# The masks of a blockwise triangular inverse: applied by VectorE as each level's product leaves PSUM, in place of GpSimd's masked copies ahead of it

## The reference

```python
def wkv_step(S, inp):
    r_t, w_t, k_t, v_t, a_t, b_t = inp
    sa = jnp.einsum('bhij,bhj->bhi', S, a_t)
    S = S * w_t[:, :, None, :] + sa[..., None] * b_t[:, :, None, :] + v_t[..., None] * k_t[:, :, None, :]
    return S, jnp.einsum('bhij,bhj->bhi', S, r_t)
...
    S_fin, y = lax.scan(wkv_step, wkv0.astype(f32), (tm(rh), tm(wh), tm(kh), tm(vh), tm(-kk), tm(kk * ah)))
```

## Time and profile before

| | |
|---|---|
| median of three runs | 1767.59 us (1760.97 to 1770.93) |
| the profiled execution | 1763.02 us, span 1761.2 us |
| mean granted TensorE clock | 0.96 |
| busy in the span: PE, PEld | 1623.6, 1501.4 us |
| busy in the span: DVE, ACT, POOL | 820.4, 587.5, 193.5 us |
| the second phase | about 316 to 795 us of the span |

### The profile page before, as it was taken

The page is one execution under the profiler, slowest core; times in us unless marked ns, Lnnn a source line. Parts: engine busy times, 40 slices in busy tenths (PEclk is TensorE's granted clock), DMA queues, the critical chain, the costliest instruction groups (busy, mean ns, idle before and its releaser), DMA issues. The chain is left out here.

```text
span 1761.2 us, 37248 instructions
## 1 busy us (share of the span) xinstructions
PE 1623.6 (92%) x15677; PEld 1501.4 (85%) x15677; DVE 820.4 (47%) x1418; ACT 587.5 (33%) x1192; POOL 193.5 (11%) x219
## 2 busy tenths in 40 slices
PE   7999995888888988883999999999999999999997
PEld 6999995666666766663998999999999999999997
DVE  5223333666677666646224244444444334444434
ACT  6433122543354544334113422222222222222211
POOL 3000000433334333222000000000000000000000
PEclk9999998988899988996999999999999999999999
DMA  6121101000000000003301111111111111111002
GB/s 170 36 53 41 48 24 34 5 3 2 2 3 3 2 3 2 3 3 96 114 25 48 48 49 48 49 40 32 48 48 48 39 32 48 48 48 48 14 11 102
DMA packets 82532, 66.79 MB, mean 38 GB/s; under 512 B 14929, under 2 KB 74507, under 8 KB 82411
## 3 DMA queue, kind: packets, MB, share of 16 engines
q1 hardware_dynamic: 79939, 64.22, 12.3%
q10 hardware_dynamic: 2408, 0.76, 0.2%
q0 software_dynamic: 64, 0.03, 0.0%
HBM read 59.63 MB, written 5.44 MB: 37 GB/s over the span
## 5 line engine op out<-in xcount | busy, mean ns | idle before, releaser
L100 PE MATMUL bank<-mix_hi,uw_hi 128*128 128x384 f32 (+1 forms) x768 | 255.7, 333 | 6.6 <-DVE uw_lo L1883 6.6
L100 PE MATMUL bank<-u_hi,dw_hi 128*128 128x384 f32 (+1 forms) x768 | 255.4, 333 | 3.6 <-DVE dw_lo L1888 3.6
L1903 DVE TENSOR_TENSOR hT<-hT,bank 128x384 f32<-128x384 f32 (+1 forms) x384 | 197.2, 535 | 131.5 <-PE bank L102 131.5
L101 PE MATMUL bank<-mix_lo,uw_hi 128*128 128x384 f32 (+1 forms) x768 | 255.1, 332 | 0.0
L102 PE MATMUL bank<-mix_hi,uw_lo 128*128 128x384 f32 (+1 forms) x768 | 255.0, 332 | 0.0
L102 PE MATMUL bank<-u_hi,dw_lo 128*128 128x384 f32 (+1 forms) x768 | 253.5, 330 | 0.0
L101 PE MATMUL bank<-u_lo,dw_hi 128*128 128x384 f32 (+1 forms) x768 | 253.5, 330 | 0.0
L1895 DVE TENSOR_TENSOR u_lo<-xn,u_hi 128x384 fp32r<-128x384 f32 (+1 forms) x96 | 52.0, 542 | 308.8 <-ACT u_hi L1854 308.8
L100 PE MATMUL bank<-x_hi,w_hi 128*128 128x384 f32 (+1 forms) x480 | 160.1, 334 | 0.0
L102 PE MATMUL bank<-x_hi,w_lo 128*128 128x384 f32 (+1 forms) x480 | 158.2, 330 | 0.0
L101 PE MATMUL bank<-x_lo,w_hi 128*128 128x384 f32 (+1 forms) x480 | 158.2, 330 | 0.0
(11 more groups left out here) (277 smaller groups left out, 2671.2 us busy)
## 6 DMA issues: line engine op xcount, KB each, us to landing
w_stage<-in_w_up SPq DMA_DIRECT2D x32, 512.0 KB, 4.5
d_stage<-in_w_down SPq DMA_DIRECT2D x32, 512.0 KB, 4.2
w_stage<-in_w_in SPq DMA_DIRECT2D x16, 512.0 KB, 3.8
proj<-in_x SPq DMA_DIRECT2D x9, 512.0 KB, 5.2
xs<-in_x SPq DMA_DIRECT2D x9, 512.0 KB, 4.7
w_stage<-in_w_in SPq DMA_DIRECT2D x8, 256.0 KB, 4.3
w_stage<-in_w_out SPq DMA_DIRECT2D x8, 256.0 KB, 2.8
w_stage<-in_w_out SPq DMA_DIRECT2D x16, 128.0 KB, 3.1
```

The source lines that it names most:

```text
L100: pe.matmul(out, hi, x_hi, start=first, stop=False)
L101: pe.matmul(out, hi, x_lo, start=False, stop=False)
L1903: dve.tensor_tensor(hT[:, m, c:c + n], hT[:, m, c:c + n], bank[j % 6][:, 0:n], ALU.add).then_inc(dn_add.sem, 1)
```

## The change

The masks are no longer applied to the triangle before the product. TensorE multiplies the unmasked triangle `Ab[:, :, 0]` with `X`, and the product is masked as it is read out of PSUM: DVE writes `Pm` = product x `lvl[:, l]`. Since `X` is block diagonal at each level, masking the product gives the same blocks, at the place that the product has them, so the constant `lvl` changes for `l` > 0: it picks the rows of the lower half and the columns of the upper one. ACT's `products` goes, GpSimd's `mask` goes with its two buffers `Ml`, and TensorE no longer waits for the mask. `products` is now the first thing in DVE's `inverse(j, l)`. GpSimd's list keeps `diagonal`, the scaling of `ys` and `prep_lx`, one behind the other after `inverse_start`.

```diff
@@ tile_heads, TensorE
             def level(j, l):
                 for g in range(2):
-                    pe.wait_ge(ml_ok.sem, ml_ok.n(j, 2 * (l - 1) + g))
...
-                    squares(f"p{l}{g}", range(4 * g, 4 * g + 4), Ml[l % 2], lambda t, h: X[t, h])
+                    squares(f"p{l}{g}", range(4 * g, 4 * g + 4), Ab[:, :, 0], lambda t, h: X[t, h])
@@ ACT
-            def products(j, l):
-                for g in range(2):
-                    act.wait_ge(f.full_of(f"p{l}{g}"), f.nth(f"p{l}{g}", j))
-                    if l > 1:
-                        act.wait_ge(f.full_of(f"t{l - 1}{g}"), f.nth(f"t{l - 1}{g}", j))
-                    act.activation(Pm[:, 4 * g:4 * g + 4], h4(out(f"p{l}{g}")[:, 0:256]), ACT.Copy).then_inc(read(f"p{l}{g}"), 1)
...
-                products(j, 1)
                 probs(j, 0)
                 if not last:
                     prep_sig(j + 1)
-                products(j, 2)
...
@@ DVE
+            def products(j, l):
+
+                for g in range(2):
+                    dve.wait_ge(f.full_of(f"p{l}{g}"), f.nth(f"p{l}{g}", j))
+                    if l > 1:
+                        dve.wait_ge(f.full_of(f"t{l - 1}{g}"), f.nth(f"t{l - 1}{g}", j))
+                    dve.tensor_tensor(Pm[:, 4 * g:4 * g + 4], h4(out(f"p{l}{g}")[:, 0:256]), lvl[:, l].unsqueeze(1).to_broadcast([P, 4, 64]),
+                                      ALU.mult).then_inc(read(f"p{l}{g}"), 1)
+
             def inverse(j, l):
+                products(j, l)
@@ GpSimd
                 inverse_start(j)
-                for l in (1, 2, 3, 4, 5):
-                    for g in range(2):
-                        mask(j, l, g)
-                    if l == 2:
-                        diagonal(j)
-                    if l == 2 and not first:
-                        pool.wait_ge(yrs.sem, yrs.n(j - 1))
-                        pool.tensor_tensor(ys[:], ys[:], yq[:], ALU.mult).then_inc(yn_ok.sem, 1)
-                    if l == 3 and not last:
-                        prep_lx(j + 1)
+                diagonal(j)
+                if not first:
+                    pool.wait_ge(yrs.sem, yrs.n(j - 1))
+                    pool.tensor_tensor(ys[:], ys[:], yq[:], ALU.mult).then_inc(yn_ok.sem, 1)
+                if not last:
+                    prep_lx(j + 1)
@@ constants
-    lvl = [((r >> (l + 1)) == (c >> (l + 1))) & (((r >> l) & 1) == 0) & (((c >> l) & 1) == 1) for l in range(6)]
+    lvl = [((r >> (l + 1)) == (c >> (l + 1))) & (((r >> l) & 1) == int(l > 0)) & (((c >> l) & 1) == int(l == 0)) for l in range(6)]
```

More of the change, by code:

```diff
@@ L477, in phase_heads @@
         X, XT, Pm = buf("X", [P, 8, 64]), buf("XT", [P, 8, 64]), buf("Pm", [P, 8, 64])
-        Ml = [buf(f"Ml{n}", [P, 8, 64]) for n in range(2)]
         WU = buf("WU", [P, 8, P])
@@ L643, in tile_heads @@
     ARs, Bt, Kt, bh, kh, Z2, L2, enL, SQ, KE, BB, elc = (v[k] for k in "ARs Bt Kt bh kh Z2 L2 enL SQ KE BB elc".split())
-    AZ, btok, ktok, vtok, Ab, Ak, X, XT, Pm, Ml, WU = (v[k] for k in "AZ btok ktok vtok Ab Ak X XT Pm Ml WU".split())
+    AZ, btok, ktok, vtok, Ab, Ak, X, XT, Pm, WU = (v[k] for k in "AZ btok ktok vtok Ab Ak X XT Pm WU".split())
     Tr, Gm, Qm, Ha, Hb, Hs, Hp, ys, yq = (v[k] for k in "Tr Gm Qm Ha Hb Hs Hp ys yq".split())
@@ L654, in tile_heads @@
     ez.per, kkrn.per, ke_ok.per = 3, 2, 2
-    xt0, xt0_ok, ml_ok, diag_ok = sem("xt0", 2), sem("xt0_ok", 2), sem("ml_ok", 10), sem("diag_ok")
+    xt0, xt0_ok, diag_ok = sem("xt0", 2), sem("xt0_ok", 2), sem("diag_ok")
     yq_ok, yrs, yn_ok, yg_ok, yb_ok = (sem(n) for n in "yq_ok yrs yn_ok yg_ok yb_ok".split())
@@ L1150, in step @@
                     prep_rn(j + 1)
-                products(j, 3)
                 if not last:
                     prep_exp(j + 1)
-                products(j, 4)
                 probs(j, 1)
                 attended(j, 0)
-                products(j, 5)
                 solved(j)
@@ L1425, in diagonal @@
                                    ALU.mult).then_inc(diag_ok.sem, 1)
[L1427 to L1432, removed]
             def inverse_start(j):
```

## The result

The changed kernel takes 1773.92 us (median of 13 runs, 1769.62 to 1783.95), the kernel before in the same comparison 1768.89 (13 runs, 1760.93 to 1770.93). The ratio is 1.0044, 95% interval [1.0026, 1.0063]: slower by 8 us by the ratio, where 31 were forecast. The sign was right, the size was not.

What follows compares the result with a forecast made beforehand. No engine is full; the path runs over TensorE and whoever makes Pm. Profiled 1763.0 + 17.6 queue + 16 clock = 1796.6, plus half of the 4.6 up to the median: 1799 us, range 1777 to 1817.

Steps and rivals of the forecast that it cites:

- Part 1: Heads, level 1: without GpSimd's 90 masks, two held VectorE operations shorten, logits ends at 432.2; without relief, 2.8 us more.
- Part 2: 90 copies move from ScalarE to VectorE, 415 ns each against 376, 0.04 us per level; the skill's figure gave 0.07.
- Part 3: Inverse levels 1 to 5: copies queue behind earlier VectorE work, step ends 2.2 us later; eight steps, 17.6 us.
- Part 4: TensorE's clock falls after the new 2.4 us wait at level 2, in four steps at 4.0 us: 16 us.
- falls of the clock that vanish: Sign of error: TensorE's clock falls disappear because a step of another length meets them otherwise; no size or chance given.
- The rivals: Alternatives for the whole kernel: delay without clock 0.26, clock falling every step (1817) 0.10, no change 0.08, faster (1752) 0.04.
- The delay alone: Queue delay of 17.6 us, level 2 wait too short to cost the clock: 1781, some 1783 at the median; chance 0.26.
- 52 us where the clock holds, of about 56 with one fall: Expected sign in the heads phase: step lengths of 52 us with clock held, about 56 with one fall, 60 with two.

Runs made afterwards that it cites:

- a_masks_fill: The changed kernel with nine spare matmuls per step before the Gm wait and GpSimd's ten mask copies per step put back, unread; 1780.03 us.
- a_fill: The changed kernel with nine spare matmuls per step ahead of TensorE's wait for Gm; 1760.68 us, ratio 0.9960 to the kernel before.
- b_long7: The kernel before with seven spare matmuls per step ahead of the second pair product, where TensorE never waits; 1771.91 us, ratio 1.0009.

## Why the prediction was wrong

- **Part 1, GpSimd's relief.** The mechanism was right, down to the 0.16 us of the two small operations, but its worth was put too low. The text said that without the relief the sum would be 2.8 us higher. That was the gain at level 1 alone; it left out that without the relief the copy would also stand behind two held operations, though the prediction's own 0.25 + 0.59 + 1.03 = 1.87 us was the figure for it. a_masks_fill shows 2.0 us per undisturbed step. The sum itself did not suffer, since it assumed the relief. The rule of the Trainium skill ("SBUF — State Buffer", Who interferes with whom) that stands there agrees with these traces: with GpSimd's copies the two operations take 0.75 and 1.19 us, without them 0.16 each, and no product of DVE took over 426 ns beside either.
- **Part 2, the copy's price.** 415 taken, 418 measured. That is 42 ns more than ScalarE's 376; the other figure given there, 0.07 us a level, did not come.
- **Part 3, the queue.** Right: 17.6 us forecast, 14.7 + 2.9 measured with the clock held in both kernels. The waits of 2.4 and 1.4 us came as worked out. That the totals agree to the tenth is luck: the first step was taken as unchanged, the middle ones too dear and the last too cheap, and these errors cancel.
- **Part 4, the clock, failed**, "four x 4.0 = 16 us", in two ways. First the size: a fall after the wait at level 2 lasts 3.4 us and costs 1.4, not 4.0. I had taken the length of the stretch after `Gm`, 10.3 us, over to another place. In the changed kernel's profile two such falls occurred, in a_fill four, the ninth step included in both. Second, and more: the term only added. It took the seven falls after the wait for `Gm` as fixed, though the price of each, 4.5 us, stood in the prediction, and though one step of eight had kept its clock. The rows behind this were read too quickly as well: of the "eight waits of 2.90 us" only three were that long, and the step of 49.6 us, said to have kept its clock "even after the long wait", had a wait of 1.68 us behind a pause of 1.01. Those 26.9 us were free to move with the step's length, and went down to 15.4. The clock's term was therefore about -11.5 and not +16. Why it went down, and not up, is not shown; b_long7 shows only that longer steps can do it without the change. Measured on the profiled executions, 33.6 us were forecast and the spans differ by 9.7, so 23.9 were missed. The clock's term was 27.5 too high and the queue 0.7 too high in these eight steps, and 4.3 us came on top outside them, 1.6 ahead of the first step and 2.7 more than the forecast's 2.2 behind the start of the last (there the clock fell once more, at level 2). The text named this under what would be wrong ("falls of the clock that vanish, since a step of another length meets them otherwise"), gave it no price and no chance, and so the range's lower end stood too high: 17.6 - 11.5 on the 1763.0 of the profiled execution is 1769, below 1777.
- **The rivals.** None of them was it. The delay alone (1781 to 1783) came nearest; the time was reached by delay and give-back together. The step lengths expected, "52 us where the clock holds, of about 56 with one fall", came as 51.4 and 54.5, but the 54.5 is a step with a fall of 6.8 us after `Gm`, and not with one of the falls at level 2 that were meant.

## What to carry to other kernels

Before a copy is given to an engine with time to spare, look at what stands ahead of it in that engine's list, not at its busy share: ten copies of 420 ns cost 1.9 us per step here, and a place a few lines higher in the list turned that into a gain. If the clock of TensorE falls in a kernel at all, compare two versions with it held, by spare matmuls in the wait that costs it; the same 17.6 us looked like 3 us in eight steps until that was done. And what the clock costs before a change is part of what a change can win or lose.

## What was not expected of the hardware

- An unbroken wait of 2.9 us for `Gm` was followed by 10.2 us at the lower clock in all three such steps of the kernel before, and by none in all three of the changed one. 14 us of added TensorE work in the phase cost 2.5 us by the medians, and double the work 26.
- 18 spare matmul records of 2.27 us per step, which nobody reads, made the kernel 31 us faster.
- A wait of 1.42 us at level 4 never cost the clock in these profiles; one of 2.39 us at level 2 did in some steps, and one of 2.07 us at level 1 in five of seven (a_masks_fill), for 3.4 us each.
